# Mixture weights of a two-layer encoder: from half matrices of expert pairs to whole matrices of one expert

## The reference, cut to what matters

```python
for e in range(N_EXPERTS):
    h = jax.nn.silu(t @ w1[e]) * (t @ w3[e])
    y = y + combine[:, e:e + 1] * (h @ w2[e])
```

## Time and profile before

| what | value |
|---|---|
| median of 3 runs | 635.6 us (635.26 to 635.79) |
| the profiled execution, its span | 634.3 us |
| TensorE (PE) busy | 620.9 us, 98% |
| moved by DMA | 229.94 MB, mean 362 GB/s |
| mixture of layer 0, from the first w1 matmul to the last scatter | 116 to 317 us |
| mixture of layer 1 | 427 to 628 us |

### The profile page before, as it was taken

One profiled execution on the slowest core, in us unless ns is written; L12 is line 12 of the kernel. 1 busy time (PEld: TensorE's weight loads), 2 busy tenths in 40 slices (PEclk: granted clock), 3 DMA queues, 4 the chain that ended last, 5 costly groups with the idle time before them and its releaser, 6 DMA issues.

```text
span 634.3 us, 10484 instructions
## 1 busy us (share of the span) xinstructions
PE 620.9 (98%) x4409; PEld 255.9 (40%) x4409; DVE 180.1 (28%) x609; ACT 139.3 (22%) x372; POOL 53.3 (8%) x61
## 2 busy tenths in 40 slices
PE   8999999999999999999999999999999999999996
PEld 5445544434324334333244454453343343343221
DVE  1665834412102102100133667343111021021011
ACT  2136642210000000000131677331100000000011
POOL 0005420000000000000010475000000000000000
PEclk9999999999999999999999999999999999999999
DMA  8999909699999999999999997697999999999993
GB/s 318 293 270 421 385 3 368 228 418 420 422 421 420 422 422 419 421 420 420 399 295 243 346 405 272 239 380 268 421 419 421 421 421 421 421 420 421 419 418 122
DMA packets 44759, 229.94 MB, mean 362 GB/s; under 512 B 8271, under 2 KB 8561, under 8 KB 21666
## 3 DMA queue, kind: packets, MB, share of 16 engines
q1 hardware_dynamic: 43068, 224.66, 90.7%
q0 software_dynamic: 1312, 4.23, 2.0%
q10 hardware_dynamic: 326, 0.31, 0.2%
HBM read 228.10 MB, written 1.08 MB: 361 GB/s over the span
## 4 chain that ended last, share of the span: by engine, by line
PE 91%; DVE 3%; ACT 2%; DMA 2%; issue 1%; POOL 0%; DVEq 0%; ACTq 0%
PE ps L1462 35%; PE ps L1474 18%; PE ps L1220 12%; PE ps L1307 8%; PE ps L1400 5%; PE ps L1431 3%; PE ps L1289 2%; PE ps L1255 2%; PE ps L1276 1%; ACT attw L572 1%; PE ps L1538 1%; PE ps L1444 1%; DMA ring<-bias_rows 1%; DMA x_sb<-in_x_dram 1%; DVE attw L872 1%
## 5 line engine op out<-in xcount | busy, mean ns | idle before, releaser
L1462 PE MATMUL ps<-attw,work 128*32 128x512 f32 x1216 | 140.1, 593 | 0.0
L1474 PE MATMUL ps<-ring,work 128*32 128x512 f32 x960 | 105.0, 593 | 0.5 <-ACT work L651 0.5
L1462 PE MATMUL ps<-ring,work 128*32 128x512 f32 x832 | 100.5, 594 | 0.0
L1220 PE MATMUL ps<-attw,work 128*128 128x512 f32 x192 | 87.4, 598 | 0.1
L1462 PEld LDWEIGHTS ps<-attw,work 128*32 128x32 f32 x1216 | 40.1, 110 | 89.1 <-issue 89.1
L1307 PE MATMUL ps<-attw,work 128*128 128x512 f32 x128 | 60.0, 602 | 0.7 <-issue 0.5
L1474 PEld LDWEIGHTS ps<-ring,work 128*32 128x32 f32 x960 | 30.3, 110 | 70.0 <-issue 68.3
L1025 DVE TENSOR_TENSOR work<-work,ps 128x256 f32<-128x256 f32 (+1 forms) x24 | 11.5, 508 | 156.0 <-PE ps L1462 156.0
L1462 PEld LDWEIGHTS ps<-ring,work 128*32 128x32 f32 x832 | 27.3, 110 | 57.6 <-issue 52.7
L1220 PEld LDWEIGHTS ps<-attw,work 128*128 128x128 f32 x192 | 34.6, 190 | 37.9 <-issue 36.9
L440 POOL TENSOR_SCALAR attw<-attw,stat 128x256 f32<-128x256 f32 x40 | 40.8, 1024 | 51.8 <-DVE stat L886 51.6
(11 more groups left out here) (161 smaller groups left out, 459.9 us busy)
## 6 DMA issues: line engine op xcount, KB each, us to landing
ring<-in_w_dram SPq DMA_DIRECT2D x112, 1024.0 KB, 26.2
attw<-in_w_dram SPq DMA_DIRECT2D x80, 1024.0 KB, 20.2
attw<-in_w_qkv_dram SPq DMA_DIRECT2D x4, 2048.0 KB, 17.4
attw<-in_w_o_dram SPq DMA_DIRECT2D x8, 1024.0 KB, 22.9
attw<-in_w_qkv_dram SPq DMA_DIRECT2D x8, 512.0 KB, 11.0
ring<-bias_rows POOLq DMA_DIRECT2D x16, 256.0 KB, 7.2
x_sb<-in_x_dram SPq DMA_DIRECT2D x2, 512.0 KB, 7.0
out_dram<-x_sb SPq DMA_DIRECT2D x2, 512.0 KB, 4.5
```

What stands on the lines that cost most here:

```text
L1220: last = pe.matmul(ps[:, g, :], xT[:, k, P * tt:P * tt + P], wqkv[part][:, k, :], start=(k == 0), stop=(k == KB - 1))
L1462: last = pe.matmul(ps[row:row + SLOTS, bank[t], :], xg[:, k, t, row:row + SLOTS], w[:, e, k % 4, :], start=(k == 0), stop=(k == KB - 1), t ...
L1474: last = pe.matmul(ps[row:row + SLOTS, bank[t], :], hT[t][:, k, row:row + SLOTS], w[:, e, k % 2, 512 * half:512 * half + 512], start=(k == ...
```

## The change

Units 4 to 45 of a layer hold one whole matrix of one expert each. Units 0 to 3 (w1 of group 0) and units 46 and 47 (w2 of the last pair) stay halves of a pair, though each is now one DMA (unit 47 two). The whole matrices are one DMA of 2 MB (units 11 and 12 two, each of two runs of 4 KB per partition, as before), 16 KB in a run for each partition. So unit j of a group is w1 of expert j, w3 of expert j - 4, w2 of expert j - 8, and the two units of a pair are needed together. A unit of w1 or w2 counts as used when both steps of its pair are done (w1 of group 0 as before); all four w3 units of a group only at the end of w3.

```diff
-        def up_unit(which, kh, p):
-            return 4 * which + 2 * kh + p
+        def up_unit(which, p, e):
+            return PER_GROUP * which + 2 * p + e
-        def down_unit(p, kh):
-            return UPS + 2 * p + kh
+        def down_unit(p, e):
+            return UPS + 2 * p + e
+        def halves_of_pairs(n):
+            return n < PER_GROUP or n >= LAST - 1
+        def up_count(n):
+            g, j = divmod(n, UNITS)
+            if j >= PER_GROUP:
+                return UPS * g + UPS
+            return UPS * g + (max(j + 1, 2) if g == 0 else 2 * (j // 2) + 2)
...
-            def load_to(dst, L, n, landed):
-                src, dst = unit_source(L, n), dst.rearrange("p (e f) -> p e f", e=2)
-                for e in range(2):
-                    sp.dma_start(dst[:, e], src[e].rearrange("p k f -> p (k f)")).then_inc(landed, 16)
+            def expert_source(L, n):
+                g, j = divmod(n, UNITS)
+                which, e = divmod(j, PER_GROUP)
+                return (w1, w3, w2)[which][L, PER_GROUP * g + e].rearrange("(p k) f -> p (k f)", p=P)
+            def load_held(L, *ns):
+                for n in ns:
+                    if halves_of_pairs(n):
+                        sp.dma_start(held[n % HELD].rearrange("p (e f) -> p e f", e=2), pair_source(L, n)).then_inc(held_landed[n % HELD], 16)
+                    else:
+                        sp.dma_start(held[n % HELD], expert_source(L, n)).then_inc(held_landed[n % HELD], 16)
...
             def wait_used(L, n):
                 if j < UPS:
-                    sp.wait_ge(main.w13_used, UPS * Q + j + 1)
+                    sp.wait_ge(main.w13_used, UPS * GROUPS * L + up_count(n))
                 else:
-                    sp.wait_ge(main.w2_used, DOWNS * Q + 2 * (j - UPS) + 2)
+                    sp.wait_ge(main.w2_used, DOWNS * (GROUPS * L + g) + 4 * ((j - UPS) // 2) + 4)
...
                     if not begun:
-                        for p in range(2):
-                            up_pair(0, 0, p)
+                        up_landed(0, 0)
+                        up_half(0, 0, 0)
+                        for t in range(TT):
+                            pe.wait_ge(m.xg_copied[t][1], Q + 1)
+                        up_half(0, 1, 0).then_inc(m.w13_used, 2)
...
+                    else:
+                        up_landed(0, 1)
+                        up_half(0, 0, 1)
...
                     for p in range(2):
-                        up_pair(1, 0, p)
-                    for p in range(2):
-                        landed(up_unit(1, 1, p))
-                        if not fetch:
+                        up_landed(1, p)
+                        up_half(1, 0, p)
+                    if not fetch:
+                        for p in range(2):
                             for k in (4, 5):
                                 up(g, 1, k, both(p), unit)
...
                     for p in range(2):
+                        by_halves = final and p == 1 and not fetch
+                        if not by_halves:
+                            for e in range(2):
+                                landed(down_unit(p, e))
```

More of the change, by code:

```diff
@@ L327, in unit_source, with load_last, wait_used @@
+            def load_last(L):
+                src, dst = pair_source(L, LAST), held[LAST % HELD].rearrange("p (e f) -> p e f", e=2)
+                for half, landed in enumerate((held_landed[LAST % HELD], last_half_landed)):
+                    part = slice(UNIT // 4 * half, UNIT // 4 * half + UNIT // 4)
+                    sp.dma_start(dst[:, :, part], src[:, :, part]).then_inc(landed, 16)
+            def wait_used(L, n):
                 g, j = divmod(n, UNITS)
                 if j < UPS:
-                    which, kh, p = j // 4, j // 2 % 2, j % 2
@@ L1460, in up, with down @@
                         row = place_of(p, e, t)
-                        w = w13_view(unit(up_unit(which, k // 4, p)))
-                        last = pe.matmul(ps[row:row + SLOTS, bank[t], :], xg[:, k, t, row:row + SLOTS], w[:, e, k % 4, :],
+                        if by_halves:
+                            w = pair_view(unit(2 * (k // 4) + p), KB)[:, e, k % 4, :]
+                        else:
+                            w = expert_view(unit(up_unit(which, p, e)), KB)[:, k, :]
+                        last = pe.matmul(ps[row:row + SLOTS, bank[t], :], xg[:, k, t, row:row + SLOTS], w,
                                          start=(k == 0), stop=(k == KB - 1), tile_position=(0, row))
                     return last
-                def down(g, p, kh, half, unit, ks=range(2)):
+                def down(g, p, kh, half, unit, ks=range(2), by_halves=False):
                     W, V = up_banks(g)
                     bank = W if half else V
-                    w = w2_view(unit(down_unit(p, kh)))
+                    cols = slice(512 * half, 512 * half + 512)
                     for k in (2 * kh + k for k in ks):
@@ L1473, in down @@
                             row = place_of(p, e, t)
-                            last = pe.matmul(ps[row:row + SLOTS, bank[t], :], hT[t][:, k, row:row + SLOTS],
-                                             w[:, e, k % 2, 512 * half:512 * half + 512],
+                            if by_halves:
+                                w = pair_view(unit(down_unit(p, kh)), FB)[:, e, k % 2, cols]
+                            else:
+                                w = expert_view(unit(down_unit(p, e)), FB)[:, k, cols]
+                            last = pe.matmul(ps[row:row + SLOTS, bank[t], :], hT[t][:, k, row:row + SLOTS], w,
                                              start=(k == 0), stop=(k == FB - 1), tile_position=(0, row))
@@ L1483, in moe_group, with up_half, up_landed @@
                     fetch = g < GROUPS - 1
-                    def up_pair(which, kh, p):
-                        landed(up_unit(which, kh, p))
+                    def up_half(which, kh, p):
                         for k in range(4 * kh, 4 * kh + 4):
-                            last = up(g, which, k, both(p), unit)
-                        last.then_inc(m.w13_used, 1)
+                            last = up(g, which, k, both(p), unit, by_halves=begun and which == 0)
+                        return last
+                    def up_landed(which, p):
+                        for e in range(2):
+                            landed(up_unit(which, p, e))
                     if g:
```

92 lines of the change are left out of this document (48 added, 44 removed).

## The result

The changed kernel takes 655.65 us (median of 4 runs, 654.11 to 656.86) beside 635.69 us before: the ratio is 1.0315, with a 95% interval of 1.0299 to 1.0330. It is slower by 20 us: slower as forecast, but by 5 us more than the 650.5 predicted, and inside the range (643.5 to 656.0) by only a third of a microsecond. The profiled execution spans 655.1 us, 20.8 more than that of before.

A forecast was written before the change was run, and what follows sets the result against it. TensorE and the DMA stream were taken as balanced, both full. Waits of 6.2 us (layer 0) and 5.9 us (layer 1) plus 2.8 us for the clock make 14.9 us on 635.6: 650.5 us, range 643.5 to 656.0.

The forecast's parts named there:

- rival 1: Weight stream: the runs of 16 KB give no gain; 654.7 us in all, chance 0.17.
- What bounds the kernel: Mixtures: TensorE and the DMA stream balanced, unit 43 only 0.2 us ahead; gain on one side worthless, loss paid in full.
- Use order of w3: w3 of group 3: unit 43 needed one step earlier, 5.0 us too late in layer 0, 5.1 in layer 1.
- Later release of w3: Group 0: units 4 to 7 freed together, DMA engines run dry, unit 15 lands 3.2 us later, 2.8 in layer 1.
- Runs of 16 KB: Weight stream: halved packets save 0.07 us per unit, 2.0 us by unit 43 in each layer.
- Rival 2: Weight stream: packets stop costing at all, 4.89 us per unit; 646.3 us, or 643.5 without the clock; chance 0.14.
- Rival 4: Stream brings unit 43 by 287.3, needing 442 GB/s, so TensorE never waits; 633.7 us, chance 0.04.
- TensorE's clock: Behind the wait of some 6 us the clock falls to half; 1.4 us per layer, between 0 and 2.9.
- Rival 3: Behind the new waits TensorE's clock doesn't fall; 647.7 us, chance 0.12.
- w2: w2 of the last group: units 44 and 45 land by 303.4, before w2 starts at 305.8, so covered.
- The bias loads: Layer 1, bias loads sharing DMA engines with units 9 and 6: taken as 0, between -1.9 and 1.6 us.

The follow-up runs named there:

- e3: Kernel before with only the loads changed: whole matrices in runs of 16 KB, order of use and releases as before; 636.47 us, ratio 1.0013.
- e12: Changed kernel with halves for w3 of first and last group and w2's first pair of the last, units 11 and 12 as four quarters each; 635.95 us.
- e2: Kernel before with the early need alone: w3's step of pair 1 already waits for units 6 and 7 of its group; 648.67 us, ratio 1.0206.
- e1: Kernel before with the late release alone: a group's four w3 units count as used together at the end of w3; 646.96 us, ratio 1.0169.
- e10: Kernel before with only the source of units 11 and 12 as changed: a half's two runs from one matrix, 8 KB apart; 639.72 us, ratio 1.0057.
- e11: Changed kernel with each half of units 11 and 12 as two DMAs of one 4 KB run per partition; 655.65 us, ratio 1.0304.
- e4: Changed kernel with each whole matrix loaded by two DMAs in runs of 8 KB; 656.93 us, ratio 1.0330.
- e9: Changed kernel with 28 matmuls that nobody reads put before the wait for unit 43 in each layer's last group; 650.48 us, ratio 1.0225.
- e6: Changed kernel with blocks 4 and 5 of w3's first pair in the last group done before the wait for unit 43; 651.14 us, ratio 1.0242.
- e8: Changed kernel with w3 of the first and last group back as halves of pairs, with former order, waits and releases; 644.25 us, ratio 1.0126.
- e7: Changed kernel with w3 of group 0 done pair after pair, so that units 4 and 5 come free earlier; 647.79 us, ratio 1.0188.

## Why the prediction was right, and where it was off

The direction and the place of the loss were right. That the time fell inside the range is luck: the upper end had been set mainly for rival 1, with a little more for the clock and the bias loads. Rival 1 didn't come true; two losses of the forecast's own mechanism, each taken too small, filled its place.

**What bounds the kernel**: right. Both sides were full, and units 41 and 43, which the prediction named, are the only ones that a matmul of the mixtures waits for, in each layer. That the wait for unit 43 is 6.2 us, as forecast, is chance: with the wait for unit 41 it is 7.3 us in layer 0 and 7.6 in layer 1, against 6.2 and 5.9. e3 and e12 show the other half of it: a gain of the stream is worth nothing.

**Use order of w3**: right, 5.0 us per layer; e2 has it alone with waits of 4.7 and a span 12.4 us longer, clock and all.

**Later release of w3**: right in place, mis-sized. 3.2 us came from "unit 15 then lands at 154.6". Its landing was forecast well (147.5 + 7.7 = 155.2, less the 0.35), but a landing is that of the slowest engine, and the stream's loss is the bytes not moved: 4.5 us in e1. In the changed kernel 3.1 us stand at the dry spell and 1.6 at a place that the prediction costed at nothing, the start of the stream. By landings alone it would look otherwise: unit 15 late by 155.2 - 0.35 - 151.4 = 3.4 us, near the forecast 3.2, and (295.1 - 155.2) / 28 = 5.00 us per unit behind it instead of the forecast 4.96. But after a dry spell the landing of unit 15 is no fair start to count from: in e1, with the runs of before, it is (296.7 - 154.6) / 28 = 5.08 us per unit, where the kernel before has 5.03.

**The start of the stream**: missed. The diff's new `load_half` takes its two runs per partition 8 KB apart from one matrix. I took it for the same DMA as before, from its equal sizes, so the sum has no term for it. e10 prices it at 639.72 - 635.87 = 3.9 us for the whole kernel where nothing covers it. In the changed kernel the dry spell covers it (e11).

**Runs of 16 KB**: 2.0 us were forecast per layer up to unit 43, and e3 measured 2.3, e4 1.6. 427 against 420 GB/s over 130 us is 2.2. So rival 1 falls. The extrapolation from halved packets held, on a thin basis: a step of 0.07 us, taken from landings read to 0.1 us. The fabric ceiling of 435 GB/s that the Trainium skill gives (DMA: Bandwidth & Descriptors, Specifications) isn't reached: 427 over a long stretch, against 420 before. Rival 2 overstated the gain: 4.89 us per unit, against 4.95 in e3. Rival 4 wanted 442 GB/s.

**TensorE's clock**: right in kind, too small. I charged 1.4 per layer between 0 and 2.9, from how soon the clock rose at the kernel's start. In the changed kernel it was down for nearly all of 294 to 301 and of 615 to 622, and e9 measured what it costs: 5.2 us in all, 2.6 per layer, near the upper bound. Rival 3 falls with it. In e2 and in layer 1 of e6 it was down for half as long. The way back is not one number.

**w2**: I costed units 44 and 45 as covered, which they were, by the wait in w3. e8 shows the price once that cover is gone, which the prediction should have given: a wait of 2.8 and 2.9 us and the clock's fall.

**The bias loads**: 0 with -1.9 and 1.6 as bounds; the two waits, 1.9 us in all, are gone, but only some 0.5 us came of it: from the first turn of x in layer 1 to the first load of its stream it was 433.4 - 317.9 = 115.5 us and is 443.8 - 328.8 = 115.0. Why it wasn't more stays open.

The sum, per layer: 5.0 for the need, 2.5 for the stream instead of 1.2, near 3 for the clock instead of 1.4. Over both layers the last two are some 5.5 us, less the 0.5 at the bias loads: the 5 us by which the forecast fell short.

## What to carry to other kernels

Where a ring of buffers between a full DMA stream and a full engine has no slack left, the grain of need and release is worth more than the size of the runs: a bigger unit must be there earlier and is given back later, and both ends showed here, at the first group (buffers full, so that releases set the stream's pace) and at the last (buffers empty, so that landings set TensorE's). Size the loss of a stream by the bytes missing in a window, not by one landing. And count a new wait of TensorE, here from 2.4 us on, with what the clock may take behind it (1.3 to 2.9 us here), and ask of each wait which later one it hides.

## What the runs showed of the hardware

- Two loads of 1 MB, each of 256 runs of 4 KB onto an idle queue, landed 5.3 us after the issue when a partition's two runs came from two matrices and 7.1 or 7.2 us when they came from one, 8 KB apart (issue 0.38 against 0.58 us; 296 against 190 GB/s over 6.5 us). The three loads of the same form right behind it landed in the same steps as those of before (3.5, 2.6 and 2.5 us behind one another in e10; 3.5, 2.5 and 2.7 before). The cause wasn't tried. Loads of one run per partition from one matrix mended only a part of it (237 GB/s in e11, 231 in e12), so the two runs in one DMA aren't the whole of it.
- A stream of 16 KB runs moved 427 GB/s where 8 KB runs moved 420.
- The granted clock fell behind TensorE's waits of 2.4 us (e4, the first wait), 2.8 (e8, both layers), 3.8 (e7) and 4.4 to 6.2 us; in e1, with 3.0 us, in layer 1 but not in layer 0; it stayed low for about 3.4 us at some places and 6.8 at others, and steps of 3.64 us took 5.0 to 6.5 us behind it.
